# Making the expert selection matrices and the first halves of the token parts ahead of a run-time branch

## The reference, cut to what matters

```
def _moe_ffn(h, router, w1, w3, w2):           # 256 tokens, 8 experts, top 2
    logits = (xt @ router).astype(jnp.float32)
    top_logit, top_idx = lax.top_k(logits, TOP_K)
    gates = jax.nn.softmax(top_logit, axis=-1)
    ...
    x_s = xt[token_s]                           # rows sorted by expert
    ...
        yb = _swiglu(xb, w1[e], w3[e], w2[e])   # only the chosen experts' rows
    ...
    out = jax.ops.segment_sum(y_s * weight_s[:, None].astype(y_s.dtype), token_s, num_segments=T)
```

## Time and profile before

| | |
|---|---|
| median of 3 runs | 1447.09 us (1446.03 to 1450.44) |
| profiled execution: its own time | 1446.48 us |
| its span (first to last instruction) | 1444.7 us |
| busy share of the span: PE, DVE, ACT, POOL | 97%, 75%, 59%, 8% |
| mean granted TensorE clock | 0.992 |

### The profile page before, as it was taken

How to read it: one execution, slowest core, us unless ns; L and a number is a source line. 1 busy time by engine, 2 the same in 40 slices (tenths; PEclk the granted TensorE clock), 3 DMA queues, 4 the chain that set the end, 5 groups by cost and what they waited for, 6 DMA issues and landing times. The chain is left out here.

```text
span 1444.7 us, 25298 instructions
## 1 busy us (share of the span) xinstructions
PE 1407.3 (97%) x10170; PEld 1227.3 (85%) x10170; DVE 1080.8 (75%) x1513; ACT 854.7 (59%) x1220; POOL 120.0 (8%) x132
## 2 busy tenths in 40 slices
PE   8999899999999999999999899999999999999999
PEld 7899788999999999988899767777777777888888
DVE  5898764765555679977566798889889888676874
ACT  4776545444444457743544677777777775447752
POOL 1057100010000001830000000000000000002000
PEclk9999999999999999999999999999999999999999
DMA  8443232445555444323244299999999998543331
GB/s 336 167 141 118 103 117 103 160 161 190 184 183 195 161 168 169 132 78 129 103 151 168 82 351 356 349 362 360 346 358 365 357 349 281 195 162 116 117 133 44
DMA packets 83527, 292.54 MB, mean 202 GB/s; under 512 B 9174, under 2 KB 13126, under 8 KB 83278
## 3 DMA queue, kind: packets, MB, share of 16 engines
q1 hardware_dynamic: 83406, 290.87, 56.2%
HBM read 289.76 MB, written 1.06 MB: 201 GB/s over the span
## 5 line engine op out<-in xcount | busy, mean ns | idle before, releaser
L402 DVE TENSOR_TENSOR ring_lo<-ring,weights_hi 128x1024 fp32r<-128x1024 f32 x345 | 424.9, 1246 | 157.0 <-ACT weights_hi L381 153.9
L381 ACT ACTIVATE weights_hi<-ring 128x1024 fp32r<-128x1024 f32 x345 | 357.8, 1055 | 164.5 <-PE bank_P L276 120.6
L274 PE MATMUL bank_P<-h_hi,weights_hi 128*128 128x256 f32 x1440 | 420.4, 292 | 1.3 <-DVE ring_lo L402 0.9
L276 PE MATMUL bank_P<-h_hi,ring_lo 128*128 128x256 f32 x1440 | 406.8, 283 | 0.0
L275 PE MATMUL bank_P<-h_lo,weights_hi 128*128 128x256 f32 x1440 | 405.6, 282 | 0.0
L274 PEld LDWEIGHTS bank_P<-h_hi,weights_hi 128*128 128x128 f32 x1440 | 272.0, 189 | 10.9 <-issue 6.9
L276 PEld LDWEIGHTS bank_P<-h_hi,ring_lo 128*128 128x128 f32 x1440 | 276.4, 192 | 0.0
L275 PEld LDWEIGHTS bank_P<-h_lo,weights_hi 128*128 128x128 f32 x1440 | 272.4, 189 | 2.3 <-issue 1.9
L275 PE MATMUL bank_P<-ring_lo,gathered_hi 128*96 128x512 f32 (+1 forms) x384 | 143.5, 374 | 0.0
L553 POOL TENSOR_TENSOR arena<-arena 128x256 f32<-128x256 f32 x98 | 97.0, 990 | 368.6 <-ACT arena L1069 356.1
L402 DVE TENSOR_TENSOR ring_lo<-ring,tokens_hi 128x1024 fp32r<-128x1024 f32 x76 | 90.3, 1215 | 0.0
(11 more groups left out here) (566 smaller groups left out, 2599.1 us busy)
## 6 DMA issues: line engine op xcount, KB each, us to landing
ring<-stream SPq DMA_DIRECT2D x541, 512.0 KB, 4.4
cst<-consts SPq DMA_DIRECT2D x1, 1520.0 KB, 17.8
arena<-x SPq DMA_DIRECT2D x2, 512.0 KB, 4.4
arena<-bias_vec SPq DMA_DIRECT2D x8, 128.0 KB, 3.0
arena<-params SPq DMA_DIRECT2D x1, 955.5 KB, 5.5
out<-arena SPq DMA_DIRECT2D x3, 256.0 KB, 2.1
arena<-params SPq DMA_DIRECT2D x2, 256.0 KB, 10.8
arena<-bias_vec SPq DMA_DIRECT2D x8, 64.0 KB, 2.7
```

Source lines behind the costliest of these rows:

```text
L274: pe.matmul(out, hi, x_hi, start=start, stop=False, skip_group_check=True)
L276: return pe.matmul(out, lo, x_hi, start=False, stop=stop, skip_group_check=True)
L381: a.activation(self.slots[i % len(self.slots)], env["ring"][:, slot, :], ACT.Copy)\
L402: v.tensor_tensor(env["ring_lo"][:, slot, :], env["ring"][:, slot, :], self.slots[i % len(self.slots)].bitcast(F32), ALU.subtract).then_in ...
```

## The change

Four instructions move from behind the branch to ahead of it: ACT's copy `htm_hi_0_1`, DVE's `htm_lo_0_1` and DVE's two `sel`. ACT makes `htm_hi_0_1` right behind `htm_hi_0_0`, ahead of the squares; DVE makes the other three at the end of routing, behind `gate_raw`. PE's gather waits for `sel` of routing and no longer for `htm_hi_0_1` or `htm_lo_0_1`, which lie ahead of the barrier. Behind the branch ACT now copies `htm_hi_1_0` and `htm_hi_1_1` first, and loads the Exp table after them, with a wait for its first Exp added.

```
@@ routing_scalar
             if half == 0:
-                a.activation(htm[0][:, 0, 0:512], tm_bank(0, 0), ACT.Copy).then_inc(*done("act", "htm_hi_0_0"))
+                for t in range(TT2):
+                    a.activation(htm[0][:, t, 0:512], tm_bank(t, 0), ACT.Copy).then_inc(*done("act", f"htm_hi_0_{t}"))
@@ token_low_parts
-        v.wait_ge(*(after(f"htm_hi_{half}_{t}", "moe") if half + t else after("squares_0_0", "routing")))
+        v.wait_ge(*(after(f"htm_hi_1_{t}", "moe") if half else after(f"squares_0_{t}", "routing")))
@@ routing_vector
         tt(dm, m2[:, :, 0], m1[:, :, 0], SUB, "gate_raw")
+        token_low_parts(v, tt, 0, 1)
+        slot_numbers = C("iota").unsqueeze(1).broadcast_to([P, EXPERTS, CAP])
+        for a in range(TT2):
+            tt(sel[:, :, a, :], slot_numbers, rank[:, a, :].unsqueeze(2).broadcast_to([P, EXPERTS, CAP]), ALU.is_equal,
+               "sel" if a else None)
@@ tensor
             if n == 0:
-                pe.wait_ge(*after("sel"))
+                pe.wait_ge(*after("sel", "routing"))
...
-            if n in (2, 3):
-                pe.wait_ge(*after("htm_lo_0_1"))
             for part in range(2):
-                if n in (0, 4):
-                    pe.wait_ge(*after((f"htm_lo_{n // 4}_1" if part else f"htm_hi_{n // 4}_1")))
+                if n == 4:
+                    pe.wait_ge(*after("htm_lo_1_1" if part else "htm_hi_1_1"))
@@ scalar
-        a.activation(dm_exp, eps("norm").broadcast_to([P, 2]), ACT.Exp).then_inc(*done("act"))
-        for half, t in ((0, 1), (1, 0), (1, 1)):
-            a.activation(htm[0][:, t, half * 512:(half + 1) * 512], tm_bank(t, half), ACT.Copy)\
-             .then_inc(*done("act", f"htm_hi_{half}_{t}"))
+        for t in range(TT2):
+            a.activation(htm[0][:, t, 512:D], tm_bank(t, 1), ACT.Copy).then_inc(*done("act", f"htm_hi_1_{t}"))
+        a.activation(dm_exp, eps("norm").broadcast_to([P, 2]), ACT.Exp).then_inc(*done("act", "exp_table"))
+        a.wait_ge(*after("exp_table"))
@@ vector
-        slot_numbers = C("iota").unsqueeze(1).broadcast_to([P, EXPERTS, CAP])
-        for a in range(TT2):
-            tt(sel[:, :, a, :], slot_numbers, rank[:, a, :].unsqueeze(2).broadcast_to([P, EXPERTS, CAP]), ALU.is_equal,
-               "sel" if a else None)
-        for half, t in ((0, 1), (1, 0), (1, 1)):
-            token_low_parts(v, tt, half, t)
+        for t in range(TT2):
+            token_low_parts(v, tt, 1, t)
```

## The result

| | before | after |
|---|---|---|
| median, 13 runs each | 1446.8 us (1445.72 to 1450.75) | 1450.6 us (1448.53 to 1453.31) |
| ratio after to before | | 1.0023, 95% interval 1.0014 to 1.0033 |
| span of the profiled execution | 1444.7 us | 1447.4 us |

The change costs about 3.3 us (0.23%; by the interval 2.0 to 4.8 us; the medians differ by 3.8). That is within the 0.3% that the prediction called no difference, but with 13 runs a side the loss is visible: the interval doesn't reach 1. Ratios leave out one run, of the experiment e6, that took 2792.22 us, nearly twice as long as all others.

A forecast was written before the change was run, and what follows sets the result against it. PE's start behind the branch was taken to hang on barrier, register load and slow jump. DVE's 0.34 + 0.73 + 1.99 us ahead of the barrier, clock 0, gave +3.1 us: 1450.2 us, range 1446.2 to 1453.8.

The forecast's parts named there:

- the clock's share: PE's slow stretch at the gather's start (clock 0.50 for 3.53 us): taken as unchanged, 0, bounds -1.6 to +1.6 us.
- The bound: PE's gap before the gather: a chain of last engine, barrier, register load and 3741 ns jump, not data.
- Rival A: PE's long jump is really a wait for data and goes away: -0.5 us, 1446.6 us; chance 0.10.
- Step 1: Routing, ahead of the barrier: ACT's copy htm_hi_0_1 ahead of the squares delays DVE's token_squares by 0.34 us.
- Steps 2 and 3: DVE ahead of the barrier: htm_lo_0_1 adds 0.73 us and the two sel 1.99 us.
- Step 4: Behind the branch: 0.73 and 1.99 us removed on DVE, 0.48 on ACT, worth nothing under PE's jump.
- Step 5: ACT behind the branch: copies, then table load and Exp; gate_exp at 802.8 us, slack 2.8 us, no cost.
- rival B: PE's longer pause doubles the slow clock stretch of the gather: +4.7 us, 1451.8 us; chance 0.12.
- Rival C: PE's jump lands in shifted code and needs a second fetch of 3.7 us: 1453.9 us; chance 0.03.

The follow-up runs named there:

- e6: Kernel before with one useless DVE sel instruction (0.98 us) added behind the branch, ahead of the two sel; ratio 0.9996 to the kernel before.
- e1: Kernel before with PE's code for overflowing experts, which is jumped over, left out so the jump is short; ratio 1.0002 to the kernel before.
- e2: Changed kernel with PE's code for overflowing experts, which is jumped over, left out so the jump is short; ratio 0.9999 to the kernel before.
- e5: Kernel before with four useless DVE sel instructions added at the end of routing, ahead of the barrier; ratio 1.0026 to the kernel before.
- e7: Kernel before without branch, register load and the barrier ahead of it, experts right behind routing; ratio 0.9981 to the kernel before.
- e8: Changed kernel without branch, register load and barrier, experts right behind routing; ratio 1.0000 to the kernel before.
- e4: Kernel before with only the two sel moved behind gate_raw, ahead of the barrier; ratio 1.0013 to the kernel before.
- e10: Changed kernel with 18 useless PE transposes added behind the rank matmuls in routing; ratio 1.0023 to the kernel before.
- e11: Kernel before with token_squares, gate_raw and the root moved from ahead of the barrier to behind the branch; ratio 0.9996 to the kernel before.

## Why the prediction was right

Measured +3.3 us (2.0 to 4.8), predicted +3.1; 1450.6 us against 1450.2. The mechanism was right, step by step as below. That the number came out within 0.2 us is in part luck, since the clock's share, taken as 0, moved the gather alone by up to 1.2 us between profiled executions.

- **The bound.** That PE's start behind the branch hangs on barrier and jump, and not on the low part that the list of waits names, is shown from five sides: the jump shrinks with the code that it skips (e1, e2), its end follows a packet of instructions by 1.4 us in all nine long jumps, work ahead of the barrier counts in full (e5), work behind it doesn't (e6), and without the branch the change costs 0.85 us in the gather's start instead of 3.0 (e7, e8). Rival A falls.
- **Step 1, ACT's copy.** `token_squares` at 795.83 us, forecast 795.84.
- **Steps 2 and 3.** `sel` ended at 798.89 us (798.92), the barrier opened at 799.3 (799.4), the gather started at 803.82 (803.93), the experts at 816.94 (817.1).
- **Step 4, the removed work is worth nothing.** Right: in the changed kernel ACT and DVE have less to do behind the branch, and PE doesn't gain by it.
- **Step 5, ACT's order behind the branch.** Wrong in the order, right in the price. I had the two copies ahead of the table load; in the trace the load of the table comes first (800.05 us), ahead of a Copy that needed none of its own in routing. It goes with the branch: in e8, without the branch, the same two copies ran first (796.53 us) and the load came behind them (797.61). The copies came 1.3 us later than I had them, and `gate_exp` at 803.88 instead of 802.8. The first split was needed at 805.48, so the slack (2.8 us by my count, 1.4 in fact) took it.
- **The clock, taken as 0.** Nearly right as a difference for the profiled pair: 3.85 us at 0.50 against 3.55, +0.14 us in the gather. There rival B's second stretch didn't come. The time alone can't exclude B, since its +4.7 us lies within the interval. For the other runs of the changed kernel the 0 isn't shown: four of the 13, the profiled one among them, had a mean granted clock of 0.990 and took 1448.53 to 1449.17 us, and nine had 0.987 to 0.989 and took 1449.42 to 1453.31. Without their traces it isn't known where the clock fell in them. Its size as noise was underrated too: gather to experts ranges from 12.69 to 13.88 us over the 13 profiles with nothing changed in PE's gather itself.
- **Rival C.** PE's jump ranged from 3.5 to 4.1 us over all kernels with the full code, with one packet on queue 8 in each; no second fetch showed.

What stays open: why the clock falls once more in the small matmuls among the first expert matmuls in six of the 13 profiled executions (e1, e2, e4, e8, e10, e11; 632.0 to 632.4 us from the experts to the end, against 630.4 to 630.8 in the others). They are the same six whose gather was slow, with 0.50 reaching 4.70 to 5.38 us into it and 13.49 to 13.88 us to the experts; in the other seven it reached 2.91 to 3.88 us, and the gather took 12.69 to 13.19. So the two go together and make some 2 us of the time, the gain of e1 among it, but no run here sets either on purpose.

## What to carry to other kernels

Work that is moved across a barrier isn't moved for free just because it stays on the same engine. Ahead of the barrier, on the engine that comes there last, all engines pay for it; behind the barrier only those that need it do. Look first for what the waiting engine itself does behind the barrier. Here its sequencer spent 3.7 us in a jump, which was cover for some 3 us of work of the others, and the list of waits blamed data that happened to be ready before its end. Read the sequencers' rows (branch, load, drain) beside the waits, and check in the code whether the named data is what the instruction needs.

## What the runs showed of the hardware

- A conditional jump took TensorE's sequencer 3.5 to 4.1 us when it skipped the section's full matmul code and 0.23 us when that code was nearly empty; the other engines, with far less code there, took 0.05 to 0.07 us. In all nine long jumps a 16 KB packet of instructions took 0.93 to 1.63 us, and the jump ended 1.4 us after it; e1 and e2 have no such packet in the jump. This agrees with the Trainium skill, "Runtime: NRT & Kernel Launch", Instruction fetch mechanics, by which a taken branch to a target outside of the window has to fetch the target's page first.
- ScalarE loaded its table again behind the branch ahead of a plain Copy (1.28 us), though in routing a Copy ran right behind the load for Sqrt, and in e8, without the branch, the same copies ran with no load ahead of them.
- TensorE's granted clock was 0.50 at the gather's first matmul in all 13 profiled executions, whose pauses before it ran from 3.6 to 10.2 us. It stayed there for 2.91 to 5.38 us of gather, and the length of the gather went with that, 12.69 to 13.88 us, not with the pause.
